# A gated recurrence with projections in its gaps: one projection tile more inside the steps of chunks 2 and 3, one fewer behind the last step

## What is computed

```python
h = rmsnorm(x, norm_mix)
p = h @ w_in                       # q_a f_a i_a g_a | qkv_b a_b b_b z_b | gate_a gate_b
# A, chunk by chunk, 4 heads:  o = PT^T v + q_dec S ;  S = decay * S + k_dec^T v
# B, chunk by chunk, 4 heads:  needs the inverse X of (I + M) of every chunk:
#     wT = (k beta e^G) X ;  v_new = X v beta - W S ;  o = q_dec S + AT v_new ;  S = g S + k_dec^T v_new
ya, yb = rmsnorm(o_a) * silu(g_a), rmsnorm(o_b) * silu(z_b)
x = x + (sigmoid(gate_a) * (ya @ w_oa) + sigmoid(gate_b) * (yb @ w_ob)) @ w_out
x = x + moe(rmsnorm(x, norm_ffn))  # top 4 of 32 experts, clamped SwiGLU
```

## Time and profile before

| | us |
|---|---|
| median of three executions | 1272.6 (1272.56 to 1274.77) |
| profiled execution, its own time | 1273.17 |
| its span, first to last instruction | 1271.4 |
| A recurrence, tile behind its step 0 to the turn of the last output | 160.8 to 214.3 |
| tiles 42 and 43 on PE | 214.3 to 221.5 |
| first matmul of wT | 221.5 |
| first update of the B state on PE | 227.0 |

### The profile page before, as it was taken

One profiled execution on the slowest core, in us unless ns is written; L12 is line 12 of the kernel. 1 busy time (PEld: TensorE's weight loads), 2 busy tenths in 40 slices (PEclk: granted clock), 3 DMA queues, 4 the chain that ended last, 5 costly groups with the idle time before them and its releaser, 6 DMA issues.

```text
span 1271.4 us, 18825 instructions
## 1 busy us (share of the span) xinstructions
PE 1210.6 (95%) x7279; PEld 541.1 (43%) x7279; DVE 509.6 (40%) x1053; ACT 242.2 (19%) x412; POOL 68.2 (5%) x156
## 2 busy tenths in 40 slices
PE   7999989989999999999999999999999999999996
PEld 5887857755533333333333333333333333333322
DVE  2184775354564333333333333334333333333344
ACT  3223511332411111111111111111111111111103
POOL 3002102001010000000000000000000000000001
PEclk9999999999999999999999999999999999999999
DMA  9343307449599999999999999999999999999995
GB/s 310 136 163 134 117 1 235 171 116 404 206 414 427 428 428 429 428 429 429 428 427 428 428 428 429 429 427 429 428 429 429 429 429 428 429 429 428 427 428 209
DMA packets 61223, 450.77 MB, mean 355 GB/s; under 512 B 9274, under 2 KB 18608, under 8 KB 36248
## 3 DMA queue, kind: packets, MB, share of 16 engines
q1 hardware_dynamic: 56484, 447.40, 85.3%
q10 hardware_dynamic: 4700, 2.83, 0.7%
HBM read 444.05 MB, written 6.26 MB: 354 GB/s over the span
## 4 chain that ended last, share of the span: by engine, by line
DMA 35%; PE 31%; DVE 3%; issue 2%; ACT 0%; SPq 0%; DVEq 0%; ACTq 0%
DMA ring<-in_w_down 35%; PE ps L1137 13%; PE ps L1169 11%; PE ps L1094 4%; PE ps L1064 1%; DVE x_tok L1980 1%; PE ps L1116 1%; DVE proj L1948 1%; DVE proj L1954 1%; PE ps L1124 0%; DVE x_tok L2052 0%; PE ps L1082 0%; PE ps L1067 0%; DVE x_tok L2041 0%; PE ps L1075 0%
## 5 line engine op out<-in xcount | busy, mean ns | idle before, releaser
L1137 PE MATMUL ps<-ring,feat 128*64 128x512 f32 x1568 | 355.5, 595 | 21.2 <-DMA ring<-in_w_gu 20.9
L1169 PE MATMUL ps<-ring,proj 128*64 128x512 f32 x992 | 238.9, 603 | 3.5 <-DMA ring<-in_w_down 3.5
L1137 PEld LDWEIGHTS ps<-ring,feat 128*64 128x64 f32 x1568 | 107.4, 136 | 205.8 <-issue 169.9
L1980 DVE TENSOR_TENSOR x_tok<-x_tok,ps 128x512 f32<-128x512 f32 x180 | 115.1, 678 | 77.2 <-PE ps L1094 77.2
L1947 DVE TENSOR_SCALAR proj<-ps 128x512 f32<-128x512 f32 x32 | 22.1, 691 | 289.9 <-PE ps L1137 289.0
L1169 PEld LDWEIGHTS ps<-ring,proj 128*64 128x64 f32 x992 | 61.2, 136 | 120.9 <-issue 104.0
L1462 ACT ACTIVATE proj<-ps,wide 128x512 f32<-128x512 f32 x32 | 22.0, 687 | 429.8 <-DVE wide L1962 424.9
L696 PE MATMUL ps<-feat,ring 128*128 128x264 f32 x384 | 93.4, 396 | 0.0
L663 PE MATMUL ps<-feat,ring 128*128 128x280 f32 (+1 forms) x384 | 90.5, 398 | 0.4 <-DVEq L1534 0.4
L663 PEld LDWEIGHTS ps<-feat,ring 128*128 128x128 f32 x384 | 72.7, 190 | 17.4 <-issue 0.5
L696 PEld LDWEIGHTS ps<-feat,ring 128*128 128x128 f32 x384 | 72.4, 194 | 15.7 <-issue 3.5
(11 more groups left out here) (403 smaller groups left out, 1122.5 us busy)
## 6 DMA issues: line engine op xcount, KB each, us to landing
ring<-in_w_gu SPq DMA_DIRECT2D x96, 2048.0 KB, 25.4
ring<-in_w_down SPq DMA_DIRECT2D x62, 2048.0 KB, 23.7
states<-in_w_gu SPq DMA_DIRECT2D x15, 2048.0 KB, 25.1
proj<-in_w_gu SPq DMA_DIRECT2D x15, 2048.0 KB, 26.3
ring<-in_w_in SPq DMA_DIRECT2D x11, 2048.0 KB, 8.7
ring<-in_w_gu SPq DMA_DIRECT2D x4, 1024.0 KB, 7.6
ring<-in_w_in SPq DMA_DIRECT2D x2, 1024.0 KB, 9.0
out<-states SPq DMA_DIRECT2D x1, 2048.0 KB, 8.7
```

Of the source, the lines that this page charges most:

```text
L1137: last = mm(bank(j // 2)[64 * (j % 2):64 * (j % 2) + 64, :], xgT[:, k % 4, k // 4, :], w[:, 512 * j:512 * j + 512], start=False, stop=k == ...
L1169: last = mm(bank(y)[64 * j:64 * j + 64, :], h[:, k % 4, 64 * (k // 4):64 * (k // 4) + 64], w[:, n:n + 512], start=False, stop=k == KT - 1)
L1980: tt(x, x, bank(5 + j)[0:r, :], ALU.add).then_inc(sg["comb_taken"], 1)
```

## The change

The tiles of the A recurrence are now taken from a counter of halves, `fill_half()`, in place of FILL[n]. Steps 2 and 3 call it three times instead of two: two halves stand ahead of the outer product and one behind it. So steps 0 to 8 hold ten tiles (33 to 42) instead of nine, and one tile, 43, is left behind the last step instead of two. Tile 36 is begun in step 2 and ended in step 3; from step 4 on each step has the tile with a number one higher. DVE, ACT, POOL and SP run the same instructions in the same order as before.

```diff
-            project_part(FILL[0], 0, 4)
+            halves = [0]
+
+            def fill_half():
+                n, second = divmod(halves[0], 2)
+                halves[0] += 1
+                project_part(FILL[0] + n, 4 * second, 4 * second + 4)
+
+            fill_half()
...
             stepA_kv(0)
-            project_part(FILL[0], 4, KT)
+            fill_half()
             for n in range(1, NCH):
...
-                project_part(FILL[n], 0, 4)
+                fill_half()
                 if n in (2, 3):
+                    fill_half()
                     pe.wait_ge(sg["stateA_upd"], H * (n + 1))
                     sample_outer(n - 2, kdA, v_diag_A).then_inc(sg["stA_outer"], 1)
-                project_part(FILL[n], 4, KT)
+                fill_half()
...
-            project(FILL[9], ONE_BANK)
+            project(FILL[0] + halves[0] // 2, ONE_BANK)
             pe.wait_ge(sg["stateA_upd"], H * NCH)
             pe.wait_ge(sg["XT_in"], 16 * H)
```

## The result

The change made the kernel slower: 1277.78 us median (1274.18 to 1280.68, 22 runs) against 1273.72 (1269.94 to 1277.23, 22 runs) of the kernel before. The ratio is 1.0034, with a 95% interval of 1.0025 to 1.0042, so it costs 0.34%, some 4.3 us. The forecast was 1274.0 from a median of 1272.6, +1.4 us, "same". A single run is worth little here: the kernel before alone spreads over 7 us in 22 runs.

The account below looks back on a forecast made before the run. It took the expert weights' DMA stream as the bound from slice 11 on, untouched but shifted by the front. Terms -0.19 and +1.57 sum to +1.38 us, giving 1274.0 from 1272.6; range 1270.9 to 1275.3.

Parts of the forecast that it names:

- the added half of step 2: Step 2 on PE: the half ahead of the outer product delays it, the add and step 3 by 1.88 us, none hidden.
- step 3 hides most of its half: Step 3 on PE: former idle time takes 1.60 of the 3.76 us filler of both steps; step 4 moves by 2.16.
- the 0.28: Step 3 on DVE: it would wait 0.28 us for PE's outer product before the second add.
- the inverses are late next: Behind the last step: the inverses' last load lands 2.16 us later, wT begins 0.8 later, PE idles some 2.3 ahead.
- My 3.46 us from store to load: SP, inverses: time from issuing the store (213.32) to issuing the loads (216.78), kept unchanged while the store moves 2.16 later.
- TensorE's clock: At the wait ahead of wT: a fall to half clock costs 1.57 us, 0 as other bound; this case had chance 0.48.
- rival D: From the wait into the B steps: clock stays low through a second stretch, +2.95 us, 1275.6; chance 0.08.
- 1.75 stretches: Half-clock time behind the wait from which the slowdown would be more than can be told from no change, about 2.5 us.
- -0.19: B's first state product on PE: at 226.83 against 227.02 before, so 0.19 us earlier if the clock holds.
- Carried whole: Behind B's first state product: nothing differs, so its shift reaches the end whole; other bound, none of it arrives.
- Rival B: At the new wait ahead of wT: the clock holds, so no 1.57 us is added, 1272.4; chance 0.31.

Follow-up runs that it names:

- chunk_early: Changed kernel with SP's load of the last w_in chunk issued ahead of the wait for the read of the sample states: 1276.46 us, 1.0021 of the kernel before.
- wide_in_wait: Changed kernel plus eight tile-sized matmuls, results unused, between tile 43 and the wait for the inverses: 1275.1 us, 1.0014 of the kernel before.
- narrow_in_wait: Changed kernel plus 60 narrow matmuls of wT's form between tile 43 and the wait for the inverses: 1278.55 us, 1.0041 of the kernel before.
- halves_behind: Changed kernel with the added halves of steps 2 and 3 behind the outer product, not ahead of it: 1274.59 us, 1.0010 of the kernel before.
- behind_and_wide: halves_behind plus the eight wide matmuls of wide_in_wait in the wait for the inverses: 1272.14 us, 0.9994 of the kernel before.
- behind_and_early: halves_behind plus the early load of the last w_in chunk from chunk_early: 1271.89 us, 0.9987 of the kernel before.
- one_half_step3: Kernel before with one half more in step 3, behind its outer product, and one half fewer behind the last step: 1275.12 us, ratio 1.0004.
- behind_wide4: halves_behind plus four wide matmuls ahead of the wait for the inverses, chunk load unmoved: 1274.68 us, 0.9997 of the kernel before.

## Why the prediction was wrong

**Right: the added half of step 2 is on the path.** Forecast +1.88 at the outer product, with 0.8 us of idle time kept ahead of step 3. Measured +1.78 (175.27 - 163.43 = 11.84 against 170.88 - 160.82 = 10.06), 0.74 kept.

**Right: step 3 hides most of its half.** Forecast +2.16 at step 4, measured +1.91. The second add did not wait on DVE (it began at 185.30, 0.05 behind the solve's operation and 0.07 behind the outer product), so the 0.28 was not there.

**Right in kind, for another reason: the inverses are late next.** Forecast: the last of their four loads 2.16 later, as the solve is. Counted from the tile of step 0, the solve's end moved by only 0.72 us, for the clock did not fall in step 5 this time, but the loads were issued at 57.73 against 55.96, +1.77. My 3.46 us from store to load was not a price of the store; it was the end of the chunk's load, which moves with the read of the sample states. chunk_early took it away and the 4.5 us became 2.4. wT began 0.43 later than before where I had 0.8, and PE idled 3.69 us where I had 2.3: the missing fall in step 5 let it come 1.6 us sooner.

**Wrong: TensorE's clock, "I take a fall: +1.57, with 0 as the other bound".** This is the step that failed, by its size: the mechanism was forecast, its length was not. I priced the fall by the one case in the trace, in which a full-width tile stood behind it and the clock came back at 197.3. Behind the new wait stand 36 narrow products, and behind them more. The clock was down for 10.2 us, and from wT to B's product PE took 8.39 us instead of the 4.53 of its own work, +3.86; less the 1.01 us of waiting for ACT that went away, and with the 0.43 at wT, that is the +3.28. wide_in_wait shows it: filler added, the delay kept, and 2.5 us come back; the two intervals overlap by 0.0004, so the time alone would be thin, but the profile has the 4.46 against 8.39. narrow_in_wait fits with why it lasted. So it was rival D, and I gave it 0.08 because "after its fall it came back at 197.3 at once, with full-width work", though I had written that narrow products follow here. Its 1.75 stretches were passed: there were three. Even D's two stretches were too few: with three the sum is -0.19 + 3 x 1.57 = +4.52, against the +3.56 at the output projection; 1.2 us of the fall lay in the wait, where it cost nothing. Besides, I started from the median of three runs, 1272.6, and that of 22 is 1273.72: 1.1 of the 3.8 us by which the forecast missed.

**The clock over all runs.** Each run has its mean granted clock. Twice what it lacks of 1, times the span, is the time at the half clock (that at the start and the end is in it):

| | runs | mean clock | us at the half clock |
|---|---|---|---|
| kernel before, three sets | 35, 34, 23 | 0.9951 to 0.9957 | 10.9 to 12.4 |
| changed kernel | 22 | 0.9922 | 20.0 |
| wide_in_wait | 12 | 0.9950 | 12.7 |
| narrow_in_wait | 12 | 0.9928 | 18.3 |
| halves_behind | 12 | 0.9933 | 17.0 |
| behind_and_wide | 12 | 0.9955 | 11.4 |

Within the sets of the kernel before, a run with more of it is longer, by 0.40 to 0.45 us for each us (correlation 0.78 to 0.84); the fall of the earlier trace rows cost 1.57 in 3.4, which is 0.46. By an estimate from these, the 7.6 to 9.1 us that the changed kernel has more cost 3.0 to 4.1 of its 4.3. In halves_behind the 5.8 more than its kernel before has would cost 2.3 to 2.6; without them it would be some 1 us faster than before, so by this estimate the tile's gain is there and the clock takes it.

**Carried whole.** The prediction carried the shift of B's first product to the end. In all ten profiles without a fall near 271, B's first state copy and the output projection are 68.97 to 68.99 us apart, so up to there it holds; behind it the profiles differ by up to 4.3 us, with falls at different places.

**Rival B by the page.** The clock fell behind a pause of 1.70 us in halves_behind, and in narrow_in_wait with PE busy. The Trainium skill, TensorE: Matmul & The Clock Gate, section HAM oscillation, tells of longer pauses alone; here the measurement decides against holding the clock by that. The pause that came, 3.69 us and not the 2.3 forecast, is a long one such as it tells of, and there the trace agrees.

**What stays open.** The move of halves_behind is worth 3.1 us by the times, which holds both the delay and the shorter falls; by the estimate above the clock has 1.2 to 1.4 of it (3.0 us less at the half clock), and the rest is the delay's or noise. With the clock held in both, wide_in_wait and behind_and_wide still differ by 2.5 us in the ratio (1.0014 and 0.9994), while their profiles have B's first state copy 0.2 us apart (65.79 and 65.58 behind A's); the intervals overlap, the clocks of all runs (12.7 and 11.4 us at the half clock) account for some 0.6 of it by the same estimate, and I can't say whether the rest is real. The profile after has also 1 us more behind the output projection's start than that before (a fall of 6.8 us near 346 where the other had 3.4 near 341); such falls came and went between kernels that are the same there, and make up part of the spread of single runs.

## What to carry to other kernels

In this kernel the idle time was room for filler only behind the last thing that somebody waits for: put the filler behind the product that another engine takes (here `sample_outer`), not ahead of it. Filler that stands in front of a round trip through DRAM may be worth more as clock than as cover; before it is taken away, ask how wide the products behind the wait are, and price the fall by them. And if a small store seems to take long, look for the large load ahead of it: moving that load brought the store here from 4.5 or 3.5 us down to 2.4.

No version here is shown to beat the kernel before. The nearest, behind_and_early, has 0.9987 (0.9972 to 1.0001).

## What the runs showed that I had not expected

- PE fully busy with 32-row products lost its full clock (3.00 of 3.00 us busy, then PEclk 0.50), and it fell too behind a pause of 1.70 us with such products after it.
- The clock stayed at 0.50 for 3.4, 6.8 or 10.2 us behind the same wait (halves_behind, one_half_step3, the changed kernel), longer the more of wT ran at it (wT took 2.39, 3.51 and 4.06 us).
- The last solve operation on DVE took 0.92 us in the changed kernel, against 0.21. POOL was busy beside both, so that alone is not the cause; in the eleven profiles with POOL busy there, one of the last two operations took 0.27 to 1.10 us and the other 0.20 or 0.21, and in behind_wide4, where POOL began only as they ended, both took 0.20:

```profile
215.65 0.92 DVE L1756 TENSOR_TENSOR ring<-ring 36x31 f32<-36x31 f32 x1
```
